# Another order in the projections' late part, and the MLP's first loads and sums placed in the attention's tail

## What is computed

```python
hn = rmsnorm(h, mix_norm[l])
a_q, a_f, a_i, a_g, b_y, b_x, c_u, d_z = jnp.split(hn @ w_in[l], IN_SPLITS, axis=-1)
...                                    # four mixers: HGRN2, RG-LRU, S5, RWKV-7
h = h + jnp.concatenate([y_a, y_b, y_c, y_d], axis=-1) @ w_out[l]
h = h + cross_attention(rmsnorm(h, xa_norm[l]), rmsnorm(mem, xa_mem_norm[l]), xa_wq[l], xa_wkv[l], xa_wo[l])
h = h + conv_ffn(rmsnorm(h, ffn_norm[l]), ffn_w_up[l], ffn_conv_w[l], ffn_conv_b[l], ffn_w_down[l])
return rmsnorm(h, final_norm)
```

## Time and profile before

| | |
|---|---|
| median of 3 runs | 3339.03 us (3336.84 to 3339.11) |
| the profiled execution's own time | 3342.05 us |
| its span in the trace | 3340.3 us |
| busy: PE, DVE, ACT, POOL | 93%, 65%, 40%, 15% |
| mean granted clock of PE | 0.962 of full |

### The profile page before, as it was taken

How to read it: one execution, slowest core, us unless ns; L and a number is a source line. 1 busy time by engine, 2 the same in 40 slices (tenths; PEclk the granted TensorE clock), 3 DMA queues, 4 the chain that set the end, 5 groups by cost and what they waited for, 6 DMA issues and landing times. The chain is left out here.

```text
span 3340.3 us, 51383 instructions
## 1 busy us (share of the span) xinstructions
PE 3090.7 (93%) x20672; PEld 2531.2 (76%) x20672; DVE 2173.6 (65%) x3314; ACT 1335.6 (40%) x2136; POOL 493.1 (15%) x650
## 2 busy tenths in 40 slices
PE   7899989699998889989999869999899998999998
PEld 6677776588887668767888758888688887778776
DVE  5666574767756557544445377767877776677776
ACT  5646555455551321112233243333433333344343
POOL 3333332557650001100000000000000000000000
PEclk9998999789999989999999989999899999999999
DMA  6262645222210264330111132323333334666774
GB/s 209 87 214 76 221 130 185 96 66 73 66 50 8 74 232 152 119 116 32 63 63 63 51 144 102 120 108 133 114 107 114 114 126 153 197 203 213 239 208 142
DMA packets 200073, 416.21 MB, mean 125 GB/s; under 512 B 15280, under 2 KB 99504, under 8 KB 193456
## 3 DMA queue, kind: packets, MB, share of 16 engines
q1 hardware_dynamic: 199856, 413.18, 37.5%
HBM read 295.66 MB, written 117.46 MB: 124 GB/s over the span
## 5 line engine op out<-in xcount | busy, mean ns | idle before, releaser
L2821 PE MATMUL ffn_ps<-ffn_t_p,ffn_w_p 128*128 128x512 f32 x3696 | 848.6, 392 | 44.1 <-DVE ffn_w_p L2997 28.5
L2821 PEld LDWEIGHTS ffn_ps<-ffn_t_p,ffn_w_p 128*128 128x128 f32 x3696 | 699.4, 189 | 193.3 <-DVE ffn_w_p L2997 30.1
L2836 PE MATMUL ffn_ps<-ffn_t_p 128*128 128x512 f32 x2112 | 490.7, 395 | 25.8 <-DVE ffn_t_p L3143 19.4
L2836 PEld LDWEIGHTS ffn_ps<-ffn_t_p 128*128 128x128 f32 x2112 | 398.3, 190 | 118.2 <-DVE ffn_t_p L3143 27.6
L481 PE MATMUL proj<-hn_high,w_high 128*128 128x512 f32 x672 | 284.6, 423 | 33.8 <-POOL w_low L397 17.1
L481 PE MATMUL proj<-hn_low,w_high 128*128 128x512 f32 x672 | 268.7, 400 | 0.0
L481 PE MATMUL proj<-hn_high,w_low 128*128 128x512 f32 x672 | 268.5, 400 | 0.0
L397 POOL TENSOR_TENSOR w_low<-w_ring,w_high 128x1024 fp32r<-128x1024 f32 x84 | 211.2, 2518 | 382.6 <-ACT w_high L525 382.6
L2847 ACT ACTIVATE ffn_w_p<-ffn_w_p_sums 128x512 fp32r<-128x512 f32 x176 | 111.2, 632 | 378.8 <-DVE ffn_w_p_sums L3018 378.7
L3143 DVE TENSOR_TENSOR ffn_t_p<-ffn_ring,ffn_t_p 128x1536 fp32r<-128x1536 f32 x88 | 154.7, 1758 | 132.1 <-ACT ffn_t_p L2917 131.6
L2917 ACT ACTIVATE ffn_t_p<-ffn_ring 128x1536 fp32r<-128x1536 f32 x88 | 131.0, 1488 | 266.2 <-DVE ffn_ring L3139 262.3
(11 more groups left out here) (477 smaller groups left out, 5849.5 us busy)
## 6 DMA issues: line engine op xcount, KB each, us to landing
ffn_ring<-in_w_up SPq DMA_DIRECT2D x44, 1024.0 KB, 5.5
ffn_ring<-in_w_down SPq DMA_DIRECT2D x88, 512.0 KB, 5.4
w_ring<-in_w_feat SPq DMA_DIRECT2D x84, 512.0 KB, 3.7
ffn_ring<-scratch_values SPq DMA_DIRECT2D x88, 257.0 KB, 4.5
scratch_gates<-ffn_gate SPq DMA_DIRECT2D x44, 512.0 KB, 2.6
ffn_ring<-scratch_gates SPq DMA_DIRECT2D x88, 256.0 KB, 3.9
scan_in<-scratch_scan SPq DMA_DIRECT2D x16, 896.0 KB, 4.5
scratch_values<-ffn_raw SPq DMA_DIRECT2D x22, 513.0 KB, 3.6
```

The lines of the kernel that those rows point to most:

```text
L2821: mm = pe.matmul(bank(name, s), w_part(name, a)[:, k * P:(k + 1) * P], t_part(name, b)[:, k * TB:(k + 1) * TB], start=k == a == b == 0, st ...
L2836: mm = pe.matmul(ps[:, DOWN_BANKS[2 * t + c]], down_part(n, x)[:, HID + t * TC:HID + (t + 1) * TC], down_part(n, y)[:, c * DH:(c + 1) * DH ...
```

## The change

In the projections:

- Product 0 of each pass goes over all blocks k with w_high by hn_high, then w_low by hn_high, then w_high by hn_low, and waits for `hn_high` in the first two thirds and `hn_ready` only in the last. The others keep their order.
- ScalarE rounds the weights of product 18 ahead of the gate's exponential of `t_ag` and those of product 19 ahead of the tanh (`high_behind(15)` and `(16)`), no longer behind the takes of 15 and 16. `norm_root` goes behind these two takes.
- `spread_rstd` moves from behind product 17 to behind product 18, and VectorE's `diagonals` from ahead of its two scans to behind them.

At the seam:

- A new function `ffn_head` lays the MLP's first buffers (operands of p5, two more raw quarters, the ring) over the place of `key_w`, and those of p6 over the attention's `hn` buffers. All other buffers move to fit.
- When the last scores are done, SP issues the MLP's first five loads. VectorE makes t1, s1, t2, t3 and the low parts of p5 between `turned_h2(14)` and the last residual; ScalarE rounds t1, s1 and t2 ahead of its last squares.
- The MLP's own head starts with s3, then s2 (made from s3 by another identity), t4, s4 and so on. The ring's slots are renumbered; SP's first load there is weights 1.

```diff
+                def steps(n):
+                    if n == 0:
+                        return [(k, i) for i in (0, 2, 1) for k in range(KT)]
+                    return [(k, i) for k in range(KT) for i in range(3)]
...
-                    for k in range(KT):
+                    for k, i in steps(n):
                         if n == 0:
-                            pe.wait_ge(*hn_ready.at(p, k))
...
+                            pe.wait_ge(*(hn_ready if i == 1 else hn_high).at(p, k))
...
-                    if n == 17 and has_next:
+                    if n == 18 and has_next:
                         spread_rstd(p + 1)
...
-                    if n + WR < NF:
-                        high(p, n + WR)
-                    elif has_next:
-                        high(p + 1, n + WR - NF)
+                    if n not in (15, 16):
+                        high_behind(n)
...
                 own.done(act.activation(T["e"][:], T["e"][:], ACT.Exp, scale=-1.0))
+                high_behind(15)
...
                 own.done(last, lb_log)
+                high_behind(16)
...
-                if has_next:
-                    norm_root(p + 1)
                 act.wait_ge(*lf_done.at(p))
                 for t in range(G2):
                     take(15 + t, T["ag"][:, t], ACT.Silu)
+                if has_next:
+                    norm_root(p + 1)
...
                 if has_next:
                     mean_square(p + 1)
-                    diagonals(p + 1)
                 for t in range(G2):
                     own.done(dve.tensor_tensor_scan(T["cum"][:, t], chunk_start, T["e"][:, t], 0.0, ALU.mult, ALU.add))
+                if has_next:
+                    diagonals(p + 1)
...
+    def load(sp):
...
+        tokens(b11, 0, 0, F["loaded"][0])
+        tokens(b12, 0, 1, F["loaded"][1])
+        sp.dma_start(w0.rearrange("p (g n) -> p g n", g=2), D["w_up"][0]).then_inc(F["loaded"][2], 16)
+        tokens(b22, 1, 1, F["beside"]["b22"])
+        tokens(raw[:, 0, 0:FFN_TURN], 1, 0, F["beside"]["b21"])
+
+    def on_act(act):
+        for what, side, name, to, sums in (("t", "t1", "p5", t5, t5_sum), ("w", "s1", "p5", w5, w5_sum), ("t", "t2", "p6", t6, t6_sum)):
+            act.wait_ge(F[what + "_added"][side], 1)
+            act.activation(to[:, 0], sums[:, 1], ACT.Copy).then_inc(F[what + "_high"][name], 1)
+
+    def on_dve(dve):
+        dve.wait_ge(F["loaded"][0], 16)
+        dve.wait_ge(F["loaded"][1], 16)
+        dve.tensor_tensor(t5_sum[:, 1], b12, b11, ALU.subtract).then_inc(F["t_added"]["t1"], 1)
+        dve.wait_ge(F["loaded"][2], 16)
+        dve.tensor_tensor(w5_sum[:, 1], a21, a22, ALU.add).then_inc(F["w_added"]["s1"], 1)
+        dve.wait_ge(F["beside"]["b22"], 16)
+        dve.wait_ge(F["t_added"]["t1"], 1)
+        dve.tensor_tensor(t6_sum[:, 1], b22, t5_sum[:, 1], ALU.subtract).then_inc(F["t_added"]["t2"], 1)
+        dve.tensor_tensor(b12, b22, b12, ALU.subtract).then_inc(F["t_added"]["t3"], 1)
+        for what, name, to, sums in (("t", "p5", t5, t5_sum), ("w", "p5", w5, w5_sum)):
+            dve.wait_ge(F[what + "_high"][name], 1)
+            dve.tensor_tensor(to[:, 1], sums[:, 1], to[:, 0], ALU.subtract).then_inc(F[what + "_split"][name], 1)
...
                 if has_two_before:
                     store_h2(i, c - 2)
+                    if not has_next:
+                        sp.wait_ge(*h3_stored.at(NCH // 2))
+                        sp.wait_ge(*S["score_done"].at(LAST))
+                        F["load"](sp)
...
-            t1_sum_first()
-            s1_sum(0)
-            t2_sum_first()
-            s2_sum(0)
-            t_sum_low("p5", 0)
-            w_sum_low("p5", 0)
+            s3_sum(0)
+            s2_sum_first()
             t4_sum(0)
...
-            t3_sum(0)
-            s3_sum(0)
```

More of the change, by code:

```diff
@@ L474, in run @@
                     pe.wait_ge(*w_split.at(p, n))
-                    for k in range(KT):
+                    for k, i in steps(n):
                         if n == 0:
-                            pe.wait_ge(*hn_ready.at(p, k))
[L478 to L482, removed]
+                            pe.wait_ge(*(hn_ready if i == 1 else hn_high).at(p, k))
+                        lhs, rhs = ((w_high, hn[0]), (w_high, hn[1]), (w_low, hn[0]))[i]
+                        mm = pe.matmul(proj[:, n % 3], lhs[:, n % WR, k * P:(k + 1) * P], rhs[:, k],
+                                       start=(k, i) == steps(n)[0], stop=(k, i) == steps(n)[-1])
+                        if n == NF - 1 and has_next and k < KT - 1 and i == 2:
                             mm.then_inc(hn_free.sem, 1)
@@ L2173, in attend_memory @@
+def attend_memory(nc, ctx, D, C, M, F):
     with ExitStack() as mem:
@@ L2295, in attend_memory @@
         NX = 4
+        assert nc.sbuf_base == F["second"]
+        hn_tok = sb("hn_tok", [P, D_MODEL])
+        hn_t = [sb(f"hn_t_{n}", [P, KT, TC], F32R) for n in ("high", "low")]
+        hn_full = sb("hn_full", [P, KT, TC])
+        assert nc.sbuf_base == F["second"] + 4 * 2 * FFN_TURN
         x_t = [sb(f"s3_x{u}", [P, D_MODEL]) for u in range(NX)]
-        hn_tok, h2_tok = sb("hn_tok", [P, D_MODEL]), sb("h2_tok", [P, D_MODEL])
+        h2_tok = sb("h2_tok", [P, D_MODEL])
         s3_junk = sb("s3_junk", [P, D_MODEL])
         ms1, ms2 = sb("ms1", [P, 1]), sb("ms2", [P, 1])
-        hn_t = [sb(f"hn_t_{n}", [P, KT, TC], F32R) for n in ("high", "low")]
-        hn_full, h3_t = sb("hn_full", [P, KT, TC]), sb("h3_t", [P, KT, TC])
+        h3_t = sb("h3_t", [P, KT, TC])
         top = sb("top", [P, XA_HEADS])
@@ L2547, in _ @@
             turned_h2(NCH - 2)
+            F["on_dve"](dve)
             residual(NCH - 1, NCH - 1)
@@ L2638, in gated_mlp @@
         gate_stored, value_stored = ([sem(f"{n}_stored{q}") for q in range(2)] for n in ("ffn_gate", "ffn_value"))
-        loaded = [sem(f"ffn_loaded{u}") for u in range(RING)]
-        beside = sems("ffn_beside", ("b21", "b22"))
+        loaded, beside = F["loaded"], F["beside"]
         down_high, down_split, down_used = sem("down_high"), sem("down_split"), sem("down_used")
@@ L2714, in load_tokens @@
                   .then_inc(loaded[load_at[what, g][0]], 16)
-            def load_beside(what):
-                sp.dma_start(tokens(what, 0).rearrange("p (k n) -> p k n", n=TB), source(what, 0)).then_inc(beside[what], 16)
             def load_down(n):
@@ L3381, in build @@
                     state_space(nc, ctx, D, C, S5, M, I)
-        for stage in (mix_out, attend_memory):
-            with nc.cleanup_on_exit():
-                stage(nc, ctx, D, C, M)
         with nc.cleanup_on_exit():
-            gated_mlp(nc, ctx, D, C)
+            mix_out(nc, ctx, D, C, M)
+        F = ffn_head(nc, D)
+        with nc.cleanup_on_exit():
+            attend_memory(nc, ctx, D, C, M, F)
+        with nc.cleanup_on_exit():
+            gated_mlp(nc, ctx, D, C, F)
 def kernel(**inputs):
```

129 lines of the change are left out of this document (84 added, 45 removed).

## The result

| | before | changed |
|---|---|---|
| median | 3339.07 us (4 runs, 3336.84 to 3342.12) | 3315.22 us (4 runs, 3311.73 to 3316.76) |
| ratio, 95% interval | | 0.9926 (0.9914 to 0.9937) |
| profiled execution, its span | 3342.05, 3340.3 | 3316.32, 3314.2 |

The change makes the kernel 23.9 us faster by the medians. The forecast was 36.0 faster (3303.0), with a range of 3292 to 3318. Both parts gave close to what was forecast; what is missing was lost in a place that the forecast took to be the same in both kernels.

The account below looks back on a forecast made before the run. TensorE, busy 93% of the span, was taken as the bound, so only its standing or half-clock time could be won. Projections 15.8 plus MLP head 20.2 gave 36.0 us: median 3303.0, own range 3298 to 3308, wide range 3292 to 3318.

Parts of the forecast that it names:

- the MLP's head: Change from attention to MLP: moved instructions and load waits leave VectorE's chain, so p7 starts 20.2 us earlier; bounds 17 to 21.
- From there on both kernels do the same, with ring slots renamed.: MLP from p7 on: the changed kernel was taken to run as before, with no gain or loss.
- the turns: Three passes' changeovers in the projections: each shrinks to 33.6 us, 13.2 saved in all; bounds 6.6 to 19.8.
- the start: Start of the projections: product 0 no longer waits for hn_low, saving 1.7 us; bounds 0 to 2.8.
- the last pass: Last pass of the projections: product 18 starts 1.8 us earlier, half is given back, saving 0.9; bounds 0 to 1.8.
- margin: Attention's end: VectorE's six moved instructions finish 1.7 us before the last residual; the chunk store's landing leaves 1 us.
- Rivals 3: MLP's head gives only 12 to 16 us, from late landing or a slow first instruction: 3309; chance 0.10.
- Rival 5: VectorE's queue ahead of the last residual: late loads make the kernel slower, 3370 at 60 GB/s; chance 0.03.
- a cold product behind product 0: Projections' turns: the next product may run at half clock, costing 2.0 us, of which 0.5 a turn was taken.
- Rival 1: Turns give little: VectorE sets their end in both kernels; 27 us faster in all, 3312; chance 0.22.
- Rival 2: Low tokens get in ahead of w_low in all turns and run unblocked; 43 us faster, 3296; chance 0.15.
- Wrong if: Signs: a turn of 37 us or more, residual later than 11.8 us, or p7 over 24 us behind the barrier.

Follow-up runs that it names:

- e2: The changed kernel with the projections' edits taken back, leaving the seam and the moved buffers; 3329.34 us, ratio 0.9960 to the kernel before.
- e3: The changed kernel with the MLP's operand addresses realigned, all seven weight and token pairs a multiple of 512 bytes apart; 3300.59 us, ratio 0.9878.
- e8: The kernel before with one 32-byte gap ahead of the MLP's weight operands; 3360.86 us, ratio 1.0062.
- e7: The kernel before with the projections' edits except product 0's new order; 3335.76 us.
- e4: The kernel before with small gaps setting different operand distances for MLP products, and the scores' and values' distances changed; 3342.62 us, ratio 1.0011.
- e9: The kernel before with 192 bytes more ahead of each of the attention's two stationary operands; 3330.94 us, ratio 0.9976.
- e1: The kernel before with only the projections' part of the change; 3327.23 us, ratio 0.9964.
- e6: The kernel before with only product 0's new order and its waits for hn_high; 3331.88 us.

## Why the prediction was right and where it failed

**The step that failed** is a sentence on the MLP's head: "From there on both kernels do the same, with ring slots renamed." Behind it stands the premise with which the forecast begins, that only time in which TensorE stands or runs at half clock can be won; time was also lost at full clock, without a wait. Both kernels do the same instructions in the same order, and TensorE stands as long in one as in the other, but it does them at another pace. The sum has no term for this: -14.1 us from p7 to the end. A second term is missing for the same reason, with the other sign: +5.9 in the attention. e2 shows both without the projections' part, e3 takes the first away with a gap of 448 bytes and one start rounded, e8 makes it in the kernel before with 32. (The stretch from p7 to the last matmul took 1362.2 us in the trace of before, 1360.1 to 1361.3 in the eight others with all seven pairs at a multiple of 256, 1376.3 in the changed kernel: against e3's 1360.9 the loss is 15.3.) With the two terms the sum becomes 36.0 + 5.9 - 14.1 = 27.8; the profiled executions differ by 25.7 (3342.05 to 3316.32), and the rest is the turns' 2.05, below; 0.7 more at the start and in the last pass and 0.7 lost between projections and attention cancel.

**The MLP's head, 20.2 forecast, 20.2 measured** (39.9 - 19.7). Its steps held: a chain of 21.1 us from barrier to p7 for 21.0 in the forecast, the loads at 388 GB/s for the 389 taken, the first matmul 0.2 us behind the first issue, the six instructions ahead of the residual in 10.1 us for 10.0, and 1.10 us of margin left for 1.7. Rivals 3 and 5 did not come about. Rival 5's place was the right one to watch: 1.1 us is all that separated the six instructions from the end of the attention.

The loads' stretch in the changed kernel:

```profile
1872.00:1876.00 4.00, 2.75 (x17) 2.12 (x15) 1.22 (x1) 0.83 (x1) 0.00 (x0) 1.00 1.05 388
1876.00:1878.00 2.00, 0.00 (x0) 0.00 (x0) 1.32 (x3) 1.98 (x5) 0.00 (x0) 1.00 1.04 339
1878.00:1880.00 2.00, 0.06 (x1) 0.09 (x2) 1.04 (x3) 0.80 (x2) 0.00 (x0) 0.92 0.43 132
```

The store of turned chunk 13 frees a buffer that VectorE asks for at 1881.13, and the wait that ends there is for TensorE. The store's own row says how near it was (a window with this transfer alone):

```profile
L2452 SPq DMA_DIRECT2D scratch_h3t<-h_t x1: 1254/1254/1254, 1868.0 to 1868.0; - x1
...
DMA to landing us min/median/max: 12.5/12.5/12.5
```

Issued at 1868.05, it landed at 1880.5, 1.5 us behind the last of the five loads (1864.17 and 14.8 us to landing: 1879.0); the store of the next chunk, with no load in front, took 3.0. By the rule of the Trainium skill that the forecast used ("DMA: Bandwidth & Descriptors", section "Queues, rings and completion order") it was to land 16 to 18 us behind the first issue of the loads, and it landed 18.6 behind it. The trace agrees as far as this; whether the store's own bytes were late too, it doesn't tell. The margin was 0.6 us where the forecast said 1.

**The turns, 13.2 forecast, 11.15 measured.** The order of events was as forecast: product 18 at 3.65 behind product 17 (3.7), no wait for `w_low`, product 0 0.65 behind the last low token (0.4), low tokens 6.97 (6.3 was taken). Two terms were too small. Product 18 took 8.35 us in the first turn (136.34 to 144.69) for 7.45: 13 of its matmuls start 427 ns apart, at half clock (1.2 GHz), where 9 did before, and the norm products wait for the spread behind it. (In e7, after the same 3.65 us of standing, it was six, in e3 none; why the number varies is open.) And GpSimd's block took 2.1 us from the low tokens, of which 1.4 were taken. Together they put the low tokens' end 1.2 us behind the forecast's 168 on its scale. The 0.5 a turn for a cold product behind product 0 did not show: product 1 took 5.8 us in the first turn, and it stands behind the mark at which a turn ends.

How much of the 2.05 is the forecast's error, one pair of traces can't say. The five traces with the old projections have the three turns at 116.4 us on average (115.5 to 117.9), the six with the new ones at 103.6 (102.8 to 104.4): 12.9 apart, close to the forecast's 13.2. The kernel before was caught at the short end, with a third turn of 36.8 where three of the other four have 38.6 to 39.9, and the changed one at the long end. One bound was also added up wrong: low tokens that end at 166.6 give a turn of 32.25, not 31.9, and 18.7 in place of 19.8.

**The start, 1.7 forecast, 2.2 measured** (product 1 from 28.74 to 26.55, with the wait for `w_low` that was named, 1.07). The trace of before was a little late here: in the six traces with the old product 0, product 1 began at 27.0 to 28.7, in the seven with the new at 26.3 to 26.8, 1.4 apart on average. **The last pass, 0.9 forecast, 1.1 left over** from 14.4.

**The rivals.** Rival 1's 3312 is nearest to the median, but not by its mechanism: the turns gave 11.15, not 6.6. Rival 2 did not happen: two of the three rows of low tokens are 6.97, and the 4.91 of the third won nothing, since the block fell just ahead of it. The forecast had named a row of 4.9 as rival 2's sign; the sign alone misleads.

**Within the range by luck.** The forecast's own range, 3298 to 3308, was missed. The wide range reaches 3315 because rivals 1 and 3 stretched it (their 3314 and 2 us more are 3316; it says 3318). Two terms that the range was not built on, -14.1 and +5.9, put the time there, and none of the three signs under "Wrong if" could have shown them.

## What to carry to other kernels

When a change moves buffers, compare the pace of the big matmul groups, not only waits and busy shares: count the matmuls in the same 100 us, or subtract starts. Write down the distance of the two operands' addresses for each matmul group, and keep it a multiple of 256 bytes; here this was worth 8 us in the attention of the kernel before and some 15 in the MLP of the changed one, for a few hundred bytes. In a turn where two engines trade places, look at what runs behind the last event, and at which clock, and do so in each turn and in more than one trace: the third turn took from 36.8 to 39.9 us in five traces with the same instructions in it.

## What the runs showed of the hardware

- Matmuls of 128x128 by 128x512 with these rounded float32 operands started 226.7 ns apart when the stationary and the moving operand were a multiple of 256 bytes apart within the partition, and 232.5 to 233.5 ns apart at 32, 64 or 128 bytes off, all at a granted clock of 1.00 (2.4 GHz). That is 3% of TensorE's time where it is the bound. It hangs on the distance, not the place: pairs that both lie 0 (p3 and p4 of the changed kernel), 192 (the MLP of the kernel before) and 224 bytes (the projections, 61,920 and 86,496) above a multiple of 256 all ran at 227. It held while VectorE and ScalarE stood idle: p1 of the changed kernel ran at 235 and 231 or 232 in turn in such a pause, from 2314.8 to 2316.0.
- The Trainium skill, "SBUF — State Buffer", section "Who interferes with whom", gives TensorE two independent read ports, one for each operand, and says that it never waits on anyone. The second speaks of other engines, and no run here contradicts it. Of two operands on independent ports one would expect that their distance plays no part, and e3, e4, e8 and e9 show that it does. What in the memory or in TensorE does it is not shown. In every slow pair the stationary operand lay 32, 64 or 128 bytes above the moving one (modulo 256); distances between 128 and 256, distances below 32, other shapes and other number formats were not tried.
- In the trace this shows only in the distances of starts, and it follows the offset: 235 and 232 in turn at 32 bytes, 236 and 231 at 64, a row of seven at 128.
- A store queued behind 5 MB of loads landed 12.5 us behind its issue, one of the same size with no load in front 3.0.
- The stretch from the first matmul behind the projections to the attention's first transposes, which no edit touches, took 865.4 us in the profiled execution of e1, 867.8 in that of e9, 869.3 in e4, 871.4 in e6 and 873.2 to 874.5 in the nine others; the cause is open, and it is why single traces are compared by stretches here.
